# Who empties the accumulator banks of the first down projection: ScalarE alone, or ScalarE and VectorE in turn

## The reference, cut to what matters

```python
def _conv_ffn(h, w_up, conv_w, conv_b, w_down):
    z = h @ w_up                          # 1024 -> 2 x 3072
    u, v = z[..., :D_FF], z[..., D_FF:]
    u = _dwconv(u, conv_w, conv_b, (1, 1))   # depthwise, width 3, over tokens
    return (jax.nn.gelu(u) * v) @ w_down     # 3072 -> 1024
```

## Time and profile before

| | us |
|---|---|
| median of 3 runs | 2160.74 |
| lowest and highest | 2158.64, 2162.23 |
| the profiled execution, its own time | 2162.23 |
| its span, first to last instruction | 2160.5 |
| mean granted TensorE clock | 0.976 |

### The profile page before, as it was taken

The page is one execution under the profiler, slowest core; times in us unless marked ns, Lnnn a source line. Parts: engine busy times, 40 slices in busy tenths (PEclk is TensorE's granted clock), DMA queues, the critical chain, the costliest instruction groups (busy, mean ns, idle before and its releaser), DMA issues.

```text
span 2160.5 us, 26604 instructions
## 1 busy us (share of the span) xinstructions
PE 2048.0 (95%) x9028; PEld 1662.8 (77%) x9028; DVE 1538.7 (71%) x1538; ACT 829.3 (38%) x1110; POOL 1276.2 (59%) x811
## 2 busy tenths in 40 slices
PE   8799999999999999999999869789999999999995
PEld 8577776777788888888888758668888888888884
DVE  6678888988677777777777784886555655566557
ACT  3475758446322222222222345562332223232322
POOL 1442334665877877787778352476765676556753
PEclk9999999998999999999999979899999999999998
DMA  7232322540222222222221400211111111111114
GB/s 283 78 109 81 116 73 83 195 147 30 97 89 93 71 87 88 92 73 87 87 89 66 166 30 11 88 59 59 39 49 58 58 49 49 49 58 49 48 39 156
DMA packets 54331, 179.68 MB, mean 83 GB/s; under 512 B 4976, under 2 KB 6288, under 8 KB 53136
## 3 DMA queue, kind: packets, MB, share of 16 engines
q1 hardware_dynamic: 54288, 179.13, 23.9%
HBM read 166.52 MB, written 12.58 MB: 83 GB/s over the span
## 4 chain that ended last, share of the span: by engine, by line
PE 80%; DVE 8%; ACT 7%; issue 3%; POOL 1%; ACTq 0%; DMA 0%; POOLq 0%; DVEq 0%
PE ps L833 39%; PE ps L553 32%; PE ps L686 3%; PE ps L936 2%; DVE Y L1785 1%; DVE sq L1705 1%; ACT TH L1131 1%; DVE X L1793 1%; PE ps L969 1%; PE ps L629 1%; DVE V L1684 1%; PE ps L601 1%; PE ps L651 1%; DVE Y L2003 1%; ACT RA L1134 1%
## 5 line engine op out<-in xcount | busy, mean ns | idle before, releaser
L1980 DVE TENSOR_TENSOR Y<-Y,ps 128x1024 f32<-128x1024 f32 x336 | 410.0, 1221 | 53.6 <-PE ps L553 13.4
L1585 POOL TENSOR_TENSOR F_lo<-S,F_hi 128x1024 fp32r<-128x1024 f32 x44 | 107.1, 2433 | 364.9 <-ACT F_hi L1266 364.9
L553 PE MATMUL ps<-F_hi,WC_hi 128*128 128x512 f32 x736 | 231.9, 393 | 3.7 <-ACT Y L1302 2.0
L1241 ACT ACTIVATE S<-S 128x1024 f32<-128x1024 f32 x48 | 50.9, 1060 | 475.1 <-DVE S L2089 475.0
L553 PE MATMUL ps<-F_hi,WC_lo 128*128 128x512 f32 x736 | 230.6, 391 | 0.0
L1029 ACT ACTIVATE So_hi<-So_raw 128x512 fp32r<-128x512 f32 x132 | 82.6, 627 | 372.7 <-POOL So_raw L1475 368.4
L553 PE MATMUL ps<-F_lo,WC_hi 128*128 128x512 f32 x704 | 218.0, 391 | 0.0
L1563 POOL TENSOR_TENSOR So_lo<-So_raw,So_hi 128x512 fp32r<-128x512 f32 x132 | 189.9, 1464 | 7.5 <-ACT So_hi L1029 7.5
L553 PEld LDWEIGHTS ps<-F_hi,WC_hi 128*128 128x128 f32 x736 | 138.8, 189 | 33.8 <-ACT Y L1302 2.7
L553 PEld LDWEIGHTS ps<-F_hi,WC_lo 128*128 128x128 f32 x736 | 139.0, 189 | 29.2
L2144 DVE TENSOR_TENSOR U<-t,ps 128x512 f32<-128x512 f32 x44 | 30.3, 688 | 178.2 <-PE ps L833 178.2
(11 more groups left out here) (288 smaller groups left out, 5366.4 us busy)
## 6 DMA issues: line engine op xcount, KB each, us to landing
rawA<-wA SPq DMA_DIRECT2D x62, 512.0 KB, 3.3
rawB<-wB SPq DMA_DIRECT2D x62, 512.0 KB, 3.3
E<-ada SPq DMA_DIRECT2D x46, 512.0 KB, 3.3
rawC<-wC SPq DMA_DIRECT2D x46, 512.0 KB, 3.4
quad<-ada SPq DMA_DIRECT2D x8, 2048.0 KB, 9.5
ada_first<-ada SPq DMA_DIRECT2D x4, 2048.0 KB, 16.5
outT<-X SPq DMA_DIRECT2D x16, 512.0 KB, 3.4
X<-outT SPq DMA_DIRECT2D x16, 512.0 KB, 7.2
```

The lines of the kernel that those rows point to most:

```text
L553: mm = pe.matmul(out, w[:, w_cols:w_cols + P], (hi, lo)[part], start=first and w is W_hi[s] and part == 0, stop=last and w is W_lo[s])
L1241: A(S[0][:], S[0][:], ACT.Gelu_apprx_tanh).then_inc(gelu_done, 1)
L1585: TT(dst[:], S[1][:], F_hi[:].bitcast(F32), ALU.subtract).then_inc(f_ready, 1)
L1980: TT(Y[:, m], Y[:, m], flat(ps[:, b:b + 2, :]), ALU.add).then_inc(d_added, 1)
```

## The change

PE, ACT, DVE and SP are all touched; POOL's stream stays as it is.

- Of the eight copies of `down(L, 0)`, ACT keeps m = 0, 2, 4, 6. DVE takes m = 1, 3, 5, 7 by a new `copy_down`. ACT no longer waits for `t_raw` nor for `ada_out` there, and copy 0 stands ahead of its roundings of "S4" and "S1".
- The DVE copies stand between pieces of DVE's own work and count in `d_added`; all later counts move by four per layer. PE waits for ACT's and DVE's copies in turn.
- "11" of step 2 now waits for ACT's four copies and DVE's first three.
- `ada_direct` moves from ahead of `down(0, 0)` to ahead of the norm of the second half of the tokens.
- SP loads the weights of step 3 ahead of the down weights of block 1, and `load_unit(4)` and (5) follow those.

```diff
@@ d_count
-            return n - 8 * (L + 1)
+            return n - 4 * (L + 1)
@@ SP, ffn
                 sp_.dma_start(raw["C"][:], wC[FJ * L]).then_inc(raw_full["C"], 16)
-                load_down(L, 1)
-                if L == 0:
-                    load_unit(4)
                 load_up(L, 3)
-                if L == 0:
-                    load_unit(5)
-                load_up(L, 4)
-                with sp_.Fori(3, FJ - 2) as j:
+                with sp_.Fori(2, FJ - 2) as j:
                     ffn_loads(L, j)
@@ PE, down
                         if m == 2:
                             pe.wait_ge(u_evac, 2 * L + 2)
-                            if L == 0:
-                                pe.wait_ge(ada_added, NH + 3)
-                        if m > 2:
-                            pe.wait_ge(d_copied, 8 * L + m - 2)
+                        if m > 2 and m % 2:
+                            pe.wait_ge(d_copied, 4 * L + m // 2)
+                        elif m > 2:
+                            pe.wait_ge(d_added, d_count(L - 1, 8 * c) + m // 2 - 1)
@@ PE, ffn_step
                 if first:
-                    pe.wait_ge(d_copied, 8 * L + 6)
+                    pe.wait_ge(d_copied, 4 * (L + 1))
+                    pe.wait_ge(d_added, d_count(L, 8 * (c - 1)) - 1)
                 quarter("11", t, first)
                 quarter("12", t, first)
+                pe.wait_ge(d_added, d_count(L, 8 * (c - 1)))
                 if first:
-                    pe.wait_ge(d_copied, 8 * (L + 1))
                     pe.wait_ge(f_mul, DN * L + 2)
@@ PE, ffn
                     ada_columns(4 * NH + 2, 2, ps[:, 6, 0:2])
+                    ada_direct(ps[:, 6, 2:4])
                 norm(2 + 4 * L, 1)
                 first_pair(L, 1)
...
-                if L == 0:
-                    pe.wait_ge(u_evac, 2)
-                    ada_direct(ps[:, 3, 0:2])
                 down(L, 0)
@@ ACT, ffn_first
                 round_t(L, 1)
-                if L == 0:
-                    act.wait_ge(ada_out, NH + 3)
-                for name in ("S4", "S1"):
+                copy_down(L, 0)
+                for name in ("S4", "S1", "11", "12"):
                     round_op(name, L, 2)
-                act.wait_ge(t_raw, 16 * (L + 1))
-                copy_down(L, 0)
-                copy_down(L, 1)
-                for name in ("11", "12"):
-                    round_op(name, L, 2)
-                for m in range(2, 6):
-                    copy_down(L, m)
+                copy_down(L, 2)
                 round_op("S2", L, 2)
+                copy_down(L, 4)
+                gelu(L, 1)
                 copy_down(L, 6)
-                gelu(L, 1)
-                copy_down(L, 7)
@@ DVE
+            def copy_down(L, m):
+                dve.wait_ge(d_done, 8 * FJ * L + m + 1)
+                dve.tensor_copy(Y[:, m], flat((AB01, AB45, AB23)[m % 3])).then_inc(d_added, 1)
...
                 right_raws(L)
-                if L == 0:
-                    add_ada_bias(ps[:, 3, 0:2], 50, 2, NH + 3)
                 right_lo(L, 0)
+                copy_down(L, 1)
                 taps(L, 1)
-                right_lo(L, 1)
+                copy_down(L, 3)
+                right_lo(L, 1, (0, 1))
+                copy_down(L, 5)
+                right_lo(L, 1, (2, 3))
                 right_lo(L, 2)
+                copy_down(L, 7)
```

More of the change, by code:

```diff
@@ L845, in ffn_step @@
                 if first:
-                    pe.wait_ge(d_copied, 8 * L + 6)
+                    pe.wait_ge(d_copied, 4 * (L + 1))
+                    pe.wait_ge(d_added, d_count(L, 8 * (c - 1)) - 1)
                 quarter("11", t, first)
                 quarter("12", t, first)
+                pe.wait_ge(d_added, d_count(L, 8 * (c - 1)))
                 if first:
-                    pe.wait_ge(d_copied, 8 * (L + 1))
                     pe.wait_ge(f_mul, DN * L + 2)
-                else:
-                    pe.wait_ge(d_added, d_count(L, 8 * (c - 1)))
-                if L == 0 and not first:
+                elif L == 0:
                     pe.wait_ge(ada_added, NH + j)
@@ L906, in ffn @@
                 if L == 0:
-                    pe.wait_ge(ada_added, NH + 2)
+                    pe.wait_ge(ada_added, NH + 3)
                 for k in range(KT):
@@ L2073, in right_raws, with right_lo @@
                 dve.wait_ge(t_raw, 16 * L + 4 * half)
-            def right_lo(L, n):
-                for k in range(KT // 2):
+            def right_lo(L, n, ks=range(KT // 2)):
+                for k in ks:
                     dve.wait_ge(t_hi, 16 * L + (0, 8, 4, 12)[n] + k + 1)
@@ L2116, in ffn_first @@
                     add_ada_bias(ps[:, 6, 0:2], 48, 2, NH + 2)
+                    add_ada_bias(ps[:, 6, 2:4], 50, 2, NH + 3)
                 right_raws(L)
-                if L == 0:
-                    add_ada_bias(ps[:, 3, 0:2], 50, 2, NH + 3)
                 right_lo(L, 0)
+                copy_down(L, 1)
                 taps(L, 1)
-                right_lo(L, 1)
+                copy_down(L, 3)
+                right_lo(L, 1, (0, 1))
+                copy_down(L, 5)
+                right_lo(L, 1, (2, 3))
                 right_lo(L, 2)
+                copy_down(L, 7)
             def ffn_step(L, j):
```

## The result

The kernel became slower. Its median was 2178.2 us over four runs, against 2159.7 over four runs of the kernel before: a ratio of 1.0084, 95% interval 1.0066 to 1.0102. The same kernel run again later, with the kernel before beside it, took 2182.5 (four runs, 2181.3 to 2184.4) against 2159.4: 1.0107, 1.0090 to 1.0124. The change costs 18 to 23 us.

A forecast was written before the change was run, and what follows sets the result against it. PE was taken as the bound (busy 2048 of 2160.5 us), with DVE the engine it waits for at the change. Layer 0 +12.0 and layer 1 +1.3 made +13.3 on the median 2160.74: 2174.0 us, range 2166 to 2181.

The forecast's parts named there:

- Term 1: DVE's four new copies from PSUM in each layer: 1.2 us each, 4.8 per layer, not slowed by POOL.
- Taking turns: DVE's `T_lo` pieces each stand behind one of POOL's: 1.70 us a piece instead of 0.60, 1.1 more.
- Term 2: Layer 1 to "S4": PE idles 7.8 us ahead of the fifth tile, "S4" 2.45 late, 1.7 regained in clock, net +0.8.
- Term 4: `ada_direct` ahead of the norm: norm 6.1 us later (bounds 4.3 and 6.9), +5.6 up to the end of block 1's unit.
- Term 5: Layer 0 to "S4": PE idles 8 us ahead of the fifth tile, "S4" at 554.9 instead of 544.25, +10.7.
- Term 3: SP's new order makes block 2's tap late for `down(1)`: +1.3 us in layer 0, +0.5 in layer 1, bounds 0 and 2.
- Relief: Rival: POOL's pieces miss DVE's `T_lo` pieces, all twelve cost 0.60 us; together -5.6, 2155; chance 6%.
- A hidden `ada_direct`: Rival: the norm waits for DVE anyway, so moving `ada_direct` costs near 0 there: 2168.4 us; chance 9%.
- Copies that take turns: Rival: DVE's copies also wait behind POOL, 2.3 us each, about +6 in all: 2180; chance 12%.

The follow-up runs named there:

- pool_pause: The changed kernel with one more wait, so ACT hands POOL nothing to subtract while DVE makes its first four `T_lo` pieces: 2174.2 us, ratio 1.0059.
- ada_only: The kernel before with only `ada_direct` moved ahead of the norm: 2166.0 us, ratio 1.0029.
- sp_only: The kernel before with only SP's new load order: 2165.7 us, ratio 1.0028.
- both_early: The kernel before with DVE's product of block 1 ahead of the last four `T_lo` pieces and ACT's first four copies not waiting for `t_raw`: 2164.5 us, 1.0010.
- e_early: The changed kernel with layer 0's E tile load (`load_unit(4)`) put ahead of step 3's A and B weights: 2175.0 us, ratio 1.0075.
- e_late: The kernel before with only layer 0's E tile load moved behind step 3's A and B weights: 2161.7 us, ratio 1.0005.
- after_ada_old: The changed kernel with `ada_direct` back at its old place ahead of `down(0, 0)`: 2173.6 us, ratio 1.0058.

## Why the prediction came out as it did

The direction, the main mechanism and, within its range, the first median (2178.2 for 2174, range 2166 to 2181) held; the second batch, 2182.5, lies above the range. The sum of the steps, +13.3, was too low: +18.5 and +23.2 were measured.

**Term 1, the copies.** 1.2 us each was taken, 1.21 to 1.23 was measured in every one, also beside POOL. Right.

**Taking turns.** Right, and shown: the first four pieces of layer 1 took 1.65 to 1.75 each in the changed kernel and 0.69 with POOL stopped, in pool_pause.

**Term 2, layer 1.** Right in every link. Shifted by the 12.1 us that this execution was behind, copy 1 ends at 1439.0 (predicted 1439.2), PE idled 7.5 (7.8), "S4" starts at 1454.0 (1454.3) at full clock, and "22" ends 0.6 later than before (0.8).

**Term 4, `ada_direct`.** Predicted +6.1 at the norm and +5.6 at the end of the unit of block 1. Measured: +6.4 and +5.3 against the profile of before; against the four profiles in which the unit of block 1 came 1.6 sooner, the second is 6.8. Right. The ada_only run shows why nothing is won at the old place: the 4.1 us that PE gains there become idle time ahead of "S4".

**Term 5, layer 0.** Predicted +10.7 at "S4". Measured against the `cnt_row` mark: +7.0 in the first profile and +9.6 in the second. The prediction had six pieces meet POOL. In the second execution six did, and the gap ahead of the fifth tile came as told (6.7 for 8). In the first only three did, since POOL's chain, held up by the load of rawB, was some 2 us later against the mark. There the fifth tile waited only 1.65 us, within the 3 us that the prediction had named as a sign of being wrong: for layer 0 of that execution its account of one long gap did not hold. The range allowed for this (three pieces more or fewer), but the text spoke of one fixed outcome where there are two.

**Term 3, SP's order, is the step that failed by its size.** It was put at +1.3 in layer 0 and +0.5 in layer 1, bounds 0 and 2. Alone it costs 5.8 (4.5 in layer 0, none in layer 1), and from "S4" to "11" of step 3 in layer 0 the changed kernel is 4.1 and 4.6 longer than before. The prediction followed only C to the tap of block 2 and let `load_unit` 4 and 5 be "part of the 1.3". It did not follow the E tile through the engines: issue (539.27 before, 557.19 after), landing, POOL's product, DVE's row sum, and the additions queued behind that sum, on whose banks "22" waits. To this comes a fall of the clock, 2.4 us in "22", which no bound held. In layer 1 the path was right: shifted by the same 12.1 us, B was issued at 1456.6 (predicted 1456.8), and ACT's tap of block 2 ran at 1469.2 (1468.6). But its size was not: a gap of 1.7 us in the second down projection in one execution and 2.3 us with a slow clock in the other, where 0.5 was predicted. The term had 1.8 where sp_only alone cost 5.8.

**How near the sum came is partly luck.** In the first profile the two stretches are 11.1 + 2.6 = 13.7 us longer than before, against 12.0 + 1.3 = 13.3 predicted. But term 5 was 3.7 too high there, while term 3 was 2.8 too low in layer 0 and 1.6 in layer 1; the errors nearly cancel. The rest of the 18.5 comes, roughly, from elsewhere: 1.2 by which this execution was behind at `cnt_row`, and 3.8 by which the two profiled executions (2162.2 and 2176.9) are closer together than the medians. In the second profile term 5 was only 1.1 too high, and the stretches are 19.0 longer.

**The rivals.** Relief would have needed `T_lo` pieces of 0.7 from the start; the first four took 1.7. Its sum of -5.6 also left out term 3; with it, it is -3.8. A hidden `ada_direct` falls with the rms activation 6.4 later. Copies that take turns fall with 1.21.

**What stays open.** Two batches of the changed kernel differ by 4.3 us. The spans of the two profiles are 4.4 apart, but that need not be the same 4.3: the mean granted clock of the profiled execution of the second batch is 0.972, as in the first batch, and that of its other three runs 0.967 to 0.968.

The stretch between layer 0 and layer 1, unedited, took from 841.2 us (ada_only) to 849.2 (both_early, e_early), 843.3 in before. The traces show where: with "11" of step 3 as the mark, every execution runs within 0.05 us of before up to 1220 us, and parts from it only in layer 1's mixer and the norms around it. The largest step, 4.3 to 4.4 us, stands at one place in e_late, e_early, both_early and after_ada_old. In e_late PE's work from the column sums at 1332 us to the matmuls that start at 1344 took 12.0 us, and the same work in before 7.7. The short gaps in it, of 0.8 and 0.9 us, are the same in both; the granted clock from 1320 to 1340 is 0.81 in e_late and 1.00 before. Why the clock fell in one and not in the other no run here shows. Such a step is almost as large as the cost of one part (5.0 to 6.2).

## What to carry to other kernels

When a load is moved in a hand-written queue, follow every tile that moves with it through each engine to the wait it can hold up, the small side tiles above all: here a late tile of modulation weights put a reduce ahead of the additions that freed a bank, and behind that wait stood a second one, for the late C. Before giving a second engine part of a job, look at what the matmuls behind it wait for: DVE was already the last to end ahead of "S4", and taking one instruction out of its way there (the product, ahead of four pieces) won 4.5 us where adding four copies lost 5.0. And where two engines contend, do not expect much from stopping one for a while: in pool_pause as many pieces were slow as without the pause. The copies that read PSUM did not suffer beside POOL in any run.

## What the runs showed of the hardware

A DVE operation with two SBUF sources took longer beside POOL (a `T_lo` piece 0.68 alone and 1.75, a tap 1.28 and 2.1 to 2.4, in the changed kernel and pool_pause), while a PSUM copy of twice a piece's elements stayed at 1.21 beside the same POOL work. The one-column f32 matmuls came every 0.11 us at a granted clock of 1.00 and every 0.22 at 0.50, which made 56 of them cost 10 us in front of a norm (the changed kernel). And the clock's loss came on top of some gaps and not of others: after the 3.5 us ahead of "22" in the changed kernel the next 12 matmuls took 5.3 us at the 1.2 GHz level, while in e_late, after a gap of 3.1, they took 2.9.
